# Attention scores of four heads per visit of TensorE, in four banks, in a fused two-layer decoder block

## The reference

```python
# layer 0
qkv = (x @ a_w_qkv[layer]).reshape(B, S, 3, A_HEADS, A_HEAD_DIM)
q = partial_rotary(qkv[:, :, 0], positions); k = partial_rotary(qkv[:, :, 1], positions)
o = moba_attention(q, k, v)                    # here: causal softmax(q k^T / 8) v
x = layer_norm(DEEPNORM_ALPHA * x + o @ a_w_o[layer], ln_g[layer, 0], ln_b[layer, 0])
# layer 1
a = attn_map(q1b, k1) - lam * attn_map(q2b, k2)
o = a @ v; o = o * rsqrt(mean(o * o) + eps) * g * (1 - lambda_init)
x = layer_norm(DEEPNORM_ALPHA * x + o @ b_w_o[j], ln_g[layer, 0], ln_b[layer, 0])
# after both
up, gate = split(x @ w_in); x = layer_norm(alpha * x + (gelu(conv(up)) * gate) @ w_out)
```

## Time and profile before

| | |
|---|---|
| median of three runs | 624.36 us |
| profiled execution | 624.4 us, span 622.6 us |
| TensorE (PE) busy | 609.9 us, 98% |
| VectorE (DVE) busy | 448.8 us, 72% |
| ScalarE (ACT) busy | 336.2 us, 54% |
| granted TensorE clock, mean | 0.996 |
| chain that ended last | 92% PE, 5% DVE, 1% DMA |

### The profile page before, as it was taken

The page is one execution under the profiler, slowest core; times in us unless marked ns, Lnnn a source line. Parts: engine busy times, 40 slices in busy tenths (PEclk is TensorE's granted clock), DMA queues, the critical chain, the costliest instruction groups (busy, mean ns, idle before and its releaser), DMA issues.

```text
span 622.6 us, 8725 instructions
## 1 busy us (share of the span) xinstructions
PE 609.9 (98%) x3316; PEld 508.8 (82%) x3316; DVE 448.8 (72%) x804; ACT 336.2 (54%) x551; POOL 53.1 (9%) x79
## 2 busy tenths in 40 slices
PE   8999999999999999999999999998999999999995
PEld 6777777798888888888877788787988888888894
DVE  4767476485777777777686676759877777777766
ACT  5778467256444455455436885863655555444530
POOL 5200000210000000000520020023000000000002
PEclk9999999999999999999999999999999999999998
DMA  8767344145666565555549443342735565655501
GB/s 308 269 249 271 136 137 138 66 151 188 202 203 204 202 199 192 185 173 192 180 154 348 137 136 135 136 136 68 265 100 193 192 201 199 203 186 178 178 1 67
DMA packets 69237, 109.83 MB, mean 176 GB/s; under 512 B 2332, under 2 KB 47692, under 8 KB 68684
## 3 DMA queue, kind: packets, MB, share of 16 engines
q1 hardware_dynamic: 68332, 105.09, 49.8%
q0 software_dynamic: 576, 4.19, 1.7%
q10 hardware_dynamic: 288, 0.00, 0.0%
HBM read 108.23 MB, written 1.05 MB: 176 GB/s over the span
## 4 chain that ended last, share of the span: by engine, by line
PE 92%; DVE 5%; DMA 1%; ACT 1%; issue 1%; DVEq 0%
PE wide L1127 16%; PE wide L1129 15%; PE wide L1128 15%; PE score L1320 11%; PE score L1322 5%; PE turn L1320 5%; PE outb L1320 5%; PE turn L1322 3%; PE outb L1322 3%; DMA raw<-in_b_w_q 1%; PE turn L1226 1%; PE turn L1194 1%; PE score L1218 1%; PE score L1215 1%; DVE xs L889 1%; DVE xT L858 1%
## 5 line engine op out<-in xcount | busy, mean ns | idle before, releaser
L841 DVE TENSOR_TENSOR w_lo<-raw,w_hi 128x2048 fp32r<-128x2048 f32 (+1 forms) x118 | 209.7, 1792 | 69.7 <-ACT w_hi L644 69.6
L644 ACT ACTIVATE w_hi<-raw 128x2048 fp32r<-128x2048 f32 (+1 forms) x126 | 182.4, 1487 | 25.2 <-PE wide L1129 19.8
L1320 PE MATMUL score<-xT,w_hi 128*128 128x512 f32 x288 | 102.6, 398 | 0.0
L1127 PE MATMUL wide<-w_hi,xT 128*128 128x512 f32 (+1 forms) x256 | 97.9, 383 | 1.0 <-DVE xT L858 0.8
L1127 PE MATMUL wide<-w_hi,oT_hi 128*128 128x512 f32 x240 | 96.2, 401 | 0.2 <-DVE oT_lo L1074 0.2
L1129 PE MATMUL wide<-w_hi,oT_lo 128*128 128x512 f32 x240 | 93.9, 391 | 0.0
L1128 PE MATMUL wide<-w_lo,oT_hi 128*128 128x512 f32 x240 | 93.6, 390 | 0.0
L1129 PE MATMUL wide<-w_hi,xT 128*128 128x512 f32 (+1 forms) x256 | 93.3, 365 | 0.0
L1128 PE MATMUL wide<-w_lo,xT 128*128 128x512 f32 (+1 forms) x256 | 93.0, 363 | 0.0
L1322 PE MATMUL score<-xT,w_lo 128*128 128x256 f32 x288 | 80.8, 280 | 0.0
L772 ACT ACTIVATE qT<-kT,conv_cols 128x256 f32<-128x256 f32 x36 | 21.8, 604 | 85.6 <-DVE kT L1040 85.6
(11 more groups left out here) (175 smaller groups left out, 877.9 us busy)
## 6 DMA issues: line engine op xcount, KB each, us to landing
raw<-in_ffn_w_in SPq DMA_DIRECT2D x44, 1024.0 KB, 5.1
raw<-in_ffn_w_out SPq DMA_DIRECT2D x22, 1024.0 KB, 4.9
raw<-in_a_w_qkv SPq DMA_DIRECT2D x9, 1024.0 KB, 5.1
raw<-in_w_kv_shared SPq DMA_DIRECT2D x8, 1024.0 KB, 5.3
raw<-in_a_w_o SPq DMA_DIRECT2D x4, 1024.0 KB, 4.8
raw<-in_b_w_q SPq DMA_DIRECT2D x4, 1024.0 KB, 5.1
raw<-in_b_w_o SPq DMA_DIRECT2D x4, 1024.0 KB, 4.9
raw<-in_a_w_qkv SPq DMA_DIRECT2D x4, 512.0 KB, 7.9
```

The lines of the kernel that those rows point to most:

```text
L644: ins = nc.scalar.activation(w_hi[c % RING][:, part], raw[c % RAW_RING][:, part], ACT.Copy)
L841: ins = nc.vector.tensor_tensor(w_lo[c % RING][:, part], raw[c % RAW_RING][:, part], w_hi[c % RING][:, part].bitcast(F32), ALU.subtract)
L1127: nc.tensor.matmul(dst, a_hi, b_hi, start=start, stop=False, skip_group_check=True)
L1320: nc.tensor.matmul(parts, w_hi[slot][:, cols], xT[:, :, kt, :], start=kt == 0, stop=False, skip_group_check=True)
```

## The change

`scores` now takes four heads in one visit, in the two score banks and `wide[2:4]`; it waits until all four masks of the previous visit are done. Projections keep four banks for the first two column groups; from the third on they use `wide[0:2]` alone, and each bank is drained by itself as soon as its token half is complete (a new semaphore `first_half_done`), instead of both by one step. In these groups four k-tiles of one token half follow each other. `wo` starts with its token half 0, whose banks wait for the halves of the last drain, and its half 1 waits for the last mask. In layer 0 `pv`, `out_hi` and `out_lo` work on heads 0 to 3, 4 to 7, 8 to 11, 12 and 13, 14 and 15; `probsT` has four buffers instead of two. In the FFN's first products the two transposes of token half 1 stand before k-tiles 5 and 7 instead of both before 6.

```diff
-    "drain": ("ACT", 0.96),
+    "drain": ("ACT", 0.5),
-    "scores": ("PE", 0.9),
+    "scores": ("PE", 1.7),
+PV_GROUPS = ((0, 1, 2, 3), (4, 5, 6, 7), (8, 9, 10, 11), (12, 13), (14, 15))
+PAIR_GROUP = [n for n, heads in enumerate(PV_GROUPS) for _ in heads[::2]]
...
-    products += [("proj", cg, kt, st) for cg in range(1, 6) for kt in range(4 if cg == 1 else 0, 8) for st in range(2)]
-    products += [("wo", kt, st, half) for kt in range(4) for st in range(2) for half in range(2)]
-    filler = [] if A else [("wo", 4, 1, 0)]
-    products += [("wo", kt, 0, half) for half in range(2) for kt in (4, 5)]
-    products += [("wo", 6, 0, half) for half in range(2)] + filler + [("wo", 7, 0, half) for half in range(2)]
-    products += [("wo", kt, 1, half) for kt in range(4, 6) for half in range(2) if ("wo", kt, 1, half) not in filler]
+    products += [("proj", 1, kt, st) for kt in range(4, 8) for st in range(2)]
+    products += [("proj", cg, 4 * h + k, st) for cg in range(2, 6) for h in range(2) for st in range(2) for k in range(4)]
+    products += [("wo", kt, st, half) for st in range(2) for half in range(2) for kt in range(4)]
+    products += [("wo", kt, 0, half) for two in ((4, 5), (6, 7)) for half in range(2) for kt in two]
+    products += [("wo", kt, 1, half) for kt in range(4, 6) for half in range(2)]
     products += [("wo", kt, 1, half) for half in range(2) for kt in range(6, 8)]
...
-        after[("drain", cg)] = [("proj", cg, 7, 1)]
-        if cg + 2 < 6:
-            after[("proj", cg + 2, 0, 0)].append(("drain", cg))
+        for st in range(2):
+            after[("drain", cg, st)] = [("proj", cg, 7, st)]
+            if cg >= 3 and cg % 3 < 2:
+                after[("drain", cg, st)].append(("qkT", cg - 3, 1))
+            if cg >= 1 and cg + 1 < 6:
+                after[("proj", cg + 1, 0, st)].append(("drain", cg if cg > 1 else 0, st))
...
+    def proj_bank(cg, st):
+        return wide[2 + st] if cg == 1 else wide[st]
...
+        score_banks = score_bank + wide[2:4]
...
-                        for st in range(ST):
-                            dst = rows[mat][:, st, :] if mat < 2 else v_rows[:, st, g * HALF:(g + 1) * HALF]
-                            nc.scalar.activation(dst, wide[2 * (m % 2) + st][:, :], ACT.Copy).then_inc(proj_drained, 1)
+                        dst = rows[mat][:, st, :] if mat < 2 else v_rows[:, st, g * HALF:(g + 1) * HALF]
+                        nc.scalar.activation(dst, proj_bank(m, st)[:, :], ACT.Copy).then_inc(proj_drained, 1)
...
-                        if kt == 0 and st == 0 and cg >= 2:
-                            pe.wait_ge(proj_drained, 12 * layer + 2 * cg - 2)
+                        if kt == 0 and cg >= 2:
+                            pe.wait_ge(proj_drained, 12 * layer + 2 * (cg - 1 if cg > 2 else 0) + st + 1)
...
                         if layer or m:
-                            pe.wait_ge(max_done, MAPS * layer + 2 * m)
-                        rows_of = [slice(0, 64), slice(64, P)]
-                        for h in range(2):
-                            qT, kT = headT[0][rows_of[h], m, :], headT[1][rows_of[h], m, :]
-                            nc.tensor.matmul(score_bank[h][:, 0:P], qT[:, 0:P], kT[:, 0:P], start=True, stop=True)
...
+                            pe.wait_ge(max_done, MAPS * layer + 4 * m)
+                        heads = [(slice(64 * (h % 2), 64 * (h % 2) + 64), 2 * m + h // 2, score_banks[h]) for h in range(4)]
+                        for two in (heads[0:2], heads[2:4]):
+                            for r, tile, scores in two:
+                                qT, kT = headT[0][r, tile, :], headT[1][r, tile, :]
+                                nc.tensor.matmul(scores[:, 0:P], qT[:, 0:P], kT[:, 0:P], start=True, stop=True)
+                            for r, tile, scores in two:
+                                qT, kT = headT[0][r, tile, :], headT[1][r, tile, :]
+                                nc.tensor.matmul(scores[:, P:3 * P], qT[:, P:2 * P], kT[:, :], start=True,
+                                                 stop=True).then_inc(scores_done, 1)
...
-                            if (st, n, kt) == (0, 1, 6):
-                                x_transposes(2 * layer + 1, (2, 3))
+                            if (st, n) == (0, 1) and kt in (5, 7):
+                                x_transposes(2 * layer + 1, (2 if kt == 5 else 3,))
```

More of the change, by code:

```diff
@@ L126, in mixer_schedule @@
         uses[c] = step
-    pair = lambda m: m // 2 if A else m
     splits = range(first_chunk + (FIRST if A else RING), first_chunk + 18)
@@ L151, in mixer_schedule @@
                 after[("qkT_out", cg, f)] = [("qkT", cg, f)]
[L152 to L155, removed]
+    for half in range(2):
+        after[("wo", 0, 0, half)].append(("drain", 5, half))
+        after[("wo", 0, 1, half)].append(("mask", 15))
     for m in range(16):
         g, f = m // 8, m // 4 % 2
-        if m % 2 == 0:
-            add(("scores", m // 2), ("qkT_out", 3 * g, f), ("qkT_out", 3 * g + 1, f), ("mask", m - 2), ("mask", m - 1))
-        add(("mask", m), ("scores", m // 2), ("exp", m - 2))
+        if m % 4 == 0:
+            add(("scores", m // 4), ("qkT_out", 3 * g, f), ("qkT_out", 3 * g + 1, f), *[("mask", n) for n in range(m - 4, m)])
+        add(("mask", m), ("scores", m // 4), ("exp", m - 2))
         add(("exp", m), ("mask", m), ("probT", m - 4 if A else m // 2 - 2))
@@ L165, in mixer_schedule @@
             add(("probT", k), ("norm", k))
[L166 to L179, removed]
+            add(("probT_out", k), ("probT", k), ("pv", PAIR_GROUP[k // 2 - 2] if A and k >= 4 else k - 2))
+        if A and m % 2 and m in [heads[-1] for heads in PV_GROUPS]:
+            n = PAIR_GROUP[m // 2]
+            add(("pv", n), *[("probT_out", h) for h in PV_GROUPS[n]], ("drain", 3 * g + 2, 1), ("out_lo", n - 1))
+            add(("out_hi", n), ("pv", n))
+            add(("out_lo", n), ("out_hi", n))
+        elif not A and m % 2:
+            add(("pv", k), ("probT_out", k), ("drain", 3 * g + 2, 1), ("pv_out", k - 1))
+            add(("pv_out", k), ("pv", k), ("subln", k - 2))
+            add(("square", k), ("pv_out", k))
+            add(("mean", k), ("square", k))
+            add(("subln", k), ("mean", k), ("outT", k - 1))
+            add(("outT", k), ("subln", k))
+            add(("out_hi", k), ("outT", k))
+            add(("out_lo", k), ("out_hi", k))
     for kt in range(8):
@@ L182, in mixer_schedule @@
             for half in range(2):
-                after[("wo", kt, st, half)].append(("out_lo", kt))
-    after[("split_hi", first_chunk + 17, 0)].append(("out_hi", 7))
+                after[("wo", kt, st, half)].append(("out_lo", PAIR_GROUP[kt] if A else kt))
+    after[("split_hi", first_chunk + 17, 0)].append(("out_hi", PAIR_GROUP[7] if A else 7))
     kinds = {}
@@ L239, in mixer_schedule @@
             takes = 1.1
-        if step[0] == "pv" and A:
-            takes = 0.9
+        if A and step[0] in ("pv", "out_hi", "out_lo") and len(PV_GROUPS[step[1]]) == 4:
+            takes = {"pv": 1.65, "out_hi": 0.5, "out_lo": 0.62}[step[0]]
+        elif A and step[0] == "pv":
+            takes = 1.0
         (products_left if step[0] in ("proj", "wo") else waiting[step[0]]).pop(0)
@@ L1276, in _ @@
                                 pe.wait_ge(lo_done, c + 1)
-                        if kt == 0 and half == 0:
-                            pe.wait_ge(proj_drained, 12 * layer + 10 + 2 * st)
+                        if kt == 0:
+                            pe.wait_ge(*((proj_drained, 12 * layer + 11 + half) if st == 0 else (max_done, MAPS * (layer + 1))))
                         rs = slice(st * P, (st + 1) * P)
```

82 lines of the change are left out of this document (44 added, 38 removed).

## The result

The changed kernel takes 619.39 us (median of six runs, 619.25 to 620.77), the kernel before in the same session 624.34 (six runs, 623.93 to 624.85): ratio 0.9928, 95% interval 0.9916 to 0.9940. That is 4.95 us less; 2.55 were forecast. The profiled execution took 619.46 us, its span is 617.7 (622.6 before).

A forecast was written before the change was run, and what follows sets the result against it. TensorE (PE) was taken as the bound: time changes only where its own work gets cheaper or its few waits change. Terms summed to -2.55 us from 624.36, forecast 621.8 us, 8-in-10 range 619.8 to 624.9.

The forecast's parts named there:

- the three costs: Layer 1: longer PE waits at second q transposes (+0.68), column group 3 (+0.50) and after the last head's transposes (+0.85).
- ten fewer entries into 64-wide work: Scores and v products in both layers: joined visits save 0.19 us per entry, -1.9 us; bounds nothing and -3.8.
- norm wait, layer 0 and 1: End of each mixer: PE's wait for the norm shrinks to about 0.1, giving -0.64 and -1.32 us.
- second FFN transposes, both layers: FFN start: a product moved ahead covers PE's wait before tokens 1, 0.36 a layer, -0.72 us for both.
- second q transposes, layer 1: They come two products after the first instead of three, so the wait grows from 0.48 to 1.16: +0.68 us.
- first product of column group 3: Layer 1, heads 0 to 7: PE waits for a bank that ScalarE drains late, about +0.5 us; bounds 0 and 1.5.
- product after the last head's transposes: Layer 1: PE waits for the last head's lower part, 0.56 + 0.29 = +0.85 us; bounds 0.3 and 1.6.
- The sentence on tiling modes: Scores and v products: if tiling changes drain TensorE, 21 changes go at 0.095, giving -2.0 instead of -1.9 us.
- The v drain: Layer 1: freeing product behind scores delays ScalarE's split, table load and exps, so the drain ends at 353.4; about +0.5 us.
- A: Rival: the second pair gains nothing in a four-head visit; 623.7 us, no measurable change; chance 0.15.
- B: Rival: two projection banks are too few, PE waits for drains at many column groups; slower, 625.6 us; chance 0.13.
- C: Rival: the three layer 1 waits are absorbed because the other engines get work earlier; 619.8 us; chance 0.15.

The follow-up runs named there:

- e1: Changed kernel with the next product put between the two pairs of heads in all eight four-head scores visits: 621.98 us.
- e4: Kernel before, with only the change's order of the last output products: 622.98 us, ratio 0.9979.
- e3: Kernel before, with only the FFN's two transposes of token half 1 split, before k-tiles 5 and 7: 623.75 us, ratio 0.9994.
- e9: Changed kernel with layer 1's drain of the first q transposes moved ahead of the second weight split on ScalarE: 618.44 us, ratio 0.9904.
- e6: Changed kernel with layer 1's first scores swapped with the product that frees the weight buffer, now ahead of them: 618.71 us, ratio 0.9911.
- e7: Changed kernel, layer 1's end: head 6's high and low part ahead of chunk 65's split on ScalarE and VectorE, head 7's transposes two products earlier: 621.13 us.

## Why the prediction was right, and where it was off

The way, the places and the three costs were forecast rightly; the size was not (4.95 us less instead of 2.55), because the joins were priced at half of what they are worth.

| term | forecast | in the trace |
|---|---|---|
| ten fewer entries into 64-wide work | -1.90 | -4.25 |
| norm wait, layer 0 and 1 | -0.64, -1.32 | -0.65, -1.33 |
| second FFN transposes, both layers | -0.72 | -0.64 |
| second q transposes, layer 1 | +0.68 | +0.72 (wait 1.20, forecast 1.16) |
| first product of column group 3 | +0.50 | +0.69 |
| product after the last head's transposes | +0.85 | +0.55 |
| `outT` 0 and `probT` 7 in layer 1 | none | +0.36, +0.12 |
| sum | -2.55 | -4.4 |

The -4.25 is eight joins of scores at 0.42 and three of v products at 0.36, less the 0.19 of the v product and scores that stood together before and no longer do. The sum in the last column agrees with the 4.4 of the table of products.

- **What bounds the kernel** was read rightly: every difference found is cheaper PE work or a longer or shorter wait of PE.
- **The term that was mis-sized** is "Ten entries fewer at 0.19" and "I take 0.19, the measured row". It is 0.42 per join of scores and 0.34 to 0.40 per join of v products. The row was that of a v product followed by scores, two kinds with 64-wide operands on different sides (128*64, then 64*128), and such a neighbourhood saves only half of what like beside like does. The upper bound of 3.8 was set at twice the same row, and was still short. The better bound stood in the earlier trace rows: a gap of 0.09 ahead, and a first group and a product start that are slower than the plain pace. Reading each start inside and behind the visit would have priced the four pieces one by one.
- **The sentence on tiling modes** counted 21 changes at 0.095. The count was right and the price was half. A visit has one change ahead of it and one behind, and the four pieces make about 0.2 us for each. Joining like with like saves two changes (0.42); a v product beside scores saves one (0.19), so that row did not show more than the rule gives but the price of one change. 21 changes at 0.19 to 0.21 give 4.0 to 4.4, where 4.25 was found. That section of the Trainium skill (TensorEngine Tiling (Array Packing), Key Properties) says that a mode change drains the array. The extra time at each edge of a visit agrees with it, and e1 brings it back; that a drain is what fills this time, no row shows.
- **End of the mixers and FFN** came out to 0.1 us; e4 and e3 show each alone, e4 also in the time, e3 only in the trace.
- **The q wait** came out at the forecast size, but its reason was only half right. The copy does stand behind a split that waits for a landing (e9). But the wait of 0.68 for this chunk is the same in nearly all traces, and what makes the q wait longer or shorter is the landing of the chunk ahead of it, which varies between executions. Nor does the landing stay where it was when PE gets earlier: the first split starts at 330.73 before and at 326.47 after, 4.26 earlier, as much as PE (4.28 in the table). The wait grew because PE comes one product sooner after the first transposes.
- **The v drain**: mechanism right (e6), 0.2 short.
- **The last head**: 0.56 was right. The other 0.29 assumed that half a split starts when the transposes do. That half began at 412.78, behind head 6's low part; the transposes came at 413.09, when PE had finished the product before them. So the half split was 0.3 ahead and cost nothing.
- **Missed**: `outT` 0 in layer 1 waits 0.36 and `probT` 7 0.12, since PE comes to them earlier. The first hangs on the same chain as the v drain: it is 0.05 in e6 and gone in e1. No experiment isolates the second.
- **Rivals.** A (no gain in the joined visit) falls with e1. B would have shown waits on drains at many column groups; there is one. C needed the three waits to be absent; they were there, and its time (619.8) was reached for another reason, the price of the joins. The plain run of products kept its pace: 0.68 us each in an unbroken run of about 15 in layer 0, before (72.08 to 81.86) and after (69.16 to 79.38).

## What to carry to other kernels

Where small matmuls of another shape stand between large ones, price them by the starts at both edges and inside, not by the visit's mean: like beside like saved both edges (0.4 us a join), unlike neighbours one (0.19). On an engine that executes a fixed list, a short drain belongs ahead of a step that waits for a transfer (e9: about 1 us gained), and a step that waits for another engine does not belong ahead of one that is ready (e7: 1.2 us lost at that place). A term that hangs on one landing carries the spread of that landing, and one trace doesn't show it.

## What the runs showed of the hardware

- Entering and leaving matmuls of 64 rows between products of 128 costs about 0.10 us at four places, 0.2 us for each change: the gap ahead, the first group (0.33 against 0.22), the last (0.53 against 0.43) and the first matmul of the product behind (0.33 against 0.23).
- The same transfer (`w_kv_shared`, layer 1) kept ScalarE waiting for 1.0 to 2.3 us in the profiled executions of the changed kernel and its nine variants (0.6 to 0.8 in the kernel before, e3 and e4), and the program's first products started up to 2.2 us apart. A wait that hangs on one landing can't be read from one trace to better than some tenths.
- ScalarE's table load took 1.28 us again and the first exp began 1.40 after its start, with one small activation between:

```profile
345.31 1.28 ACT L725 ACT_TABLE_LOAD   x1
...
346.71 0.39 ACT L733 ACTIVATE probs<-masked,neg_max 128x128 f32<-128x128 f32 x1
```
